# A small clock of step times sets the order inside three mixers; gate products move ahead in the queue; weight slabs are halved

## The reference

```python
for l in range(2):                                     # first block: two hybrid layers
    h = layer_norm(ALPHA*x + 0.5*swiglu(x, ffn1), ...)
    q,k,v,b,a,z, sw_q,sw_k,sw_v, xa_q, gates = split(h @ w_in)
    o_dn = gated_delta_rule(...)                       # 4 heads, chunks, triangular solve, state chain
    o_sw = sliding_window_attention(...)               # 8 heads in 4 pairs, window 128, sink logits
    o_xa = memory_cross_attention(...)                 # 4 heads over 256 memory rows
    merged = sum_n sigmoid(gates_n) * (branch_n @ w_branch_n)
    h = layer_norm(ALPHA*h + merged @ w_out)
    x = layer_norm(ALPHA*h + 0.5*swiglu(h, ffn2))
x = x + token_mixer(rmsnorm(x))                        # second block: four attentions, 4 heads each:
                                                       # stick-breaking (sb), blocks with T5 bias (mb),
                                                       # forgetting (fx), top-256 keys (ds)
x = x + conv_ffn(rmsnorm(x)); out = rmsnorm(x)
```

## Time and profile before

| | us |
|---|---|
| median of 3 runs | 3833.05 (3832.97 to 3834.43) |
| the profiled execution: its own time | 3830.93 |
| its span, first to last instruction | 3829.2 |
| PE busy | 3677.4 (96%) |
| DVE busy | 1879.4 (49%) |
| ACT busy | 1383.5 (36%) |
| mean granted TensorE clock | 0.981 |

### The profile page before, as it was taken

How to read it: one execution, slowest core, us unless ns; L and a number is a source line. 1 busy time by engine, 2 the same in 40 slices (tenths; PEclk the granted TensorE clock), 3 DMA queues, 4 the chain that set the end, 5 groups by cost and what they waited for, 6 DMA issues and landing times.

```text
span 3829.2 us, 42473 instructions
## 1 busy us (share of the span) xinstructions
PE 3677.4 (96%) x16966; PEld 2905.5 (76%) x16966; DVE 1879.4 (49%) x3117; ACT 1383.5 (36%) x2292; POOL 0.2 (0%) x4
## 2 busy tenths in 40 slices
PE   8999989999999999999899999999999998999998
PEld 6888768777778887888688768788857676778887
DVE  4333575563543344334665654533254567646643
ACT  4332363442242223222644432422234333334432
POOL 0000000000000000000000000000000000000000
PEclk9999999999999999999999999999989999999999
DMA  4322210112222222222110112222222112122222
GB/s 152 121 99 95 81 61 34 44 56 83 86 85 94 94 94 83 94 94 93 66 45 23 67 61 94 77 99 91 97 76 74 55 61 77 67 88 88 96 97 77
DMA packets 88316, 308.26 MB, mean 81 GB/s; under 512 B 9846, under 2 KB 12055, under 8 KB 87992
## 3 DMA queue, kind: packets, MB, share of 16 engines
q1 hardware_dynamic: 88120, 305.55, 23.0%
HBM read 300.80 MB, written 4.72 MB: 80 GB/s over the span
## 4 chain that ended last, share of the span: by engine, by line
PE 86%; DVE 8%; ACT 4%; issue 1%; DMA 0%; DVEq 0%; SPq 0%; ACTq 0%
PE bank L1569 25%; PE bank L1570 25%; PE bank L1571 25%; PE bank L1552 4%; PE bank L1604 1%; DVE page_f L2329 1%; PE bank L1557 1%; DVE w_lo L2153 1%; PE bank L1579 1%; ACT w_hi L1826 1%; ACT L1810 0%; PE bank L1624 0%; DVE small L2277 0%; PE bank L1779 0%; ACT page_f L1973 0%
## 5 line engine op out<-in xcount | busy, mean ns | idle before, releaser
L1569 PE MATMUL bank<-page_r,w_hi 128*128 128x512 f32 (+1 forms) x4488 | 1817.5, 405 | 50.0 <-DVE page_r L2184 26.6
L1570 PE MATMUL bank<-page_r,w_hi 128*128 128x512 f32 (+1 forms) x4488 | 1768.9, 394 | 0.0
L1571 PE MATMUL bank<-page_r,w_lo 128*128 128x512 f32 (+1 forms) x4488 | 1768.5, 394 | 0.0
L1569 PEld LDWEIGHTS bank<-page_r,w_hi 128*128 128x128 f32 x4488 | 850.1, 189 | 274.5 <-issue 69.3
L2153 DVE TENSOR_TENSOR w_lo<-raw,w_hi 128x1024 fp32r<-128x1024 f32 x561 | 685.6, 1223 | 696.9 <-ACT w_hi L1826 696.8
L1571 PEld LDWEIGHTS bank<-page_r,w_lo 128*128 128x128 f32 x4488 | 849.2, 189 | 199.0
L1570 PEld LDWEIGHTS bank<-page_r,w_hi 128*128 128x128 f32 x4488 | 850.7, 190 | 186.1 <-issue 4.6
L1826 ACT ACTIVATE w_hi<-raw 128x1024 fp32r<-128x1024 f32 x561 | 590.7, 1054 | 792.8 <-PE bank L1571 791.1
L2253 DVE TENSOR_TENSOR page_f<-page_f,bank 128x512 f32<-128x512 f32 x88 | 60.6, 689 | 261.4 <-PE bank L1571 255.0
L1898 ACT ACTIVATE page_r<-page_f 128x512 fp32r<-128x512 f32 x88 | 55.7, 633 | 354.4 <-DVE page_f L2253 354.4
L1552 PEld LDWEIGHTS bank<-page_f 128*128 128x128 f32 x1344 | 165.1, 193 | 14.5 <-DVE page_f L2422 4.2
(11 more groups left out here) (212 smaller groups left out, 2216.5 us busy)
## 6 DMA issues: line engine op xcount, KB each, us to landing
raw<-weights SPq DMA_DIRECT2D x561, 512.0 KB, 3.2
page_f<-x_t SPq DMA_DIRECT2D x8, 256.0 KB, 4.3
bias_rows<-page_f SPq DMA_DIRECT2D x8, 256.0 KB, 2.0
page_f<-bias_rows SPq DMA_DIRECT2D x8, 256.0 KB, 3.3
out_t<-page_f SPq DMA_DIRECT2D x8, 256.0 KB, 2.1
cst<-consts SPq DMA_DIRECT2D x1, 1088.0 KB, 6.9
page_f<-mem_t SPq DMA_DIRECT2D x8, 128.0 KB, 5.6
bias_rows<-page_f SPq DMA_DIRECT2D x8, 64.0 KB, 1.9
```

Of the source, the lines that this page charges most:

```text
L1569: self.e.matmul(o, hi, X.hi[kt], start=first, stop=False)
L1570: self.e.matmul(o, hi, X.lo[kt], start=False, stop=False)
L1571: last = self.e.matmul(o, lo, X.hi[kt], start=False, stop=final)
```

## The change

1. **Slabs of 4 blocks.** 1122 slabs of 128x512. Six raw buffers, four rounded ones. The remainder is written over the raw slab (`w_lo` is the same memory as `raw`), so a raw buffer is free only when PE has multiplied its slab, and SP waits for that. Rounding of slab s+3 stands at block 1 of slab s, its remainder at block 2, the load of slab s+5 at block 0. Pages go from 76 to 84.
2. **A clock.** Each yield now returns an estimate: PE time, a list of DVE and ACT times, and whether the next step needs the result. `Pace` keeps the time of PE (`now`) and of DVE and ACT (`free`). `weave` takes a lane whose next step is ready by `now` plus 0.1, else a ready step of the queue, else whatever is ready first. A yield may also return a flag or another generator to wait for, so each lane goes on by itself.
3. **No common ends.** Hybrid: lane one is decays, head 0, head 2, cross heads 0-1; lane two head 1, head 3, window pairs 0-1; cross heads 2-3 start after head 2, window pairs 2-3 after head 3. Second block: a lane for each head pair goes through sb, mb, fx, ds; the ranking is a lane. All projections but the first four are queue work.
4. **Gates.** The delta output gates are products of the queue before the heads end, and `gate_ahead(n)` puts the eight gate products of a merge into the queue ahead of it, so the last merge has only its branch products (32 blocks) left.

```diff
-NSLAB = 561
-NRAW = 3
-NSPLIT = 3
-AHEAD = NSPLIT - 1
-PAGES = 76
-N_SB, N_MB, N_FX, N_DS = 2.4, 1.9, 2.3, 1.8
+SLAB = 4
+NSLAB = 1122
+NRAW = 6
+NHI = 4
+AHEAD = NHI - 1
+PAGES = 84
+BLOCK_US = 0.7
+LAG_US = 0.1
...
+def vec(width, n=1):
+    return (("V", 0.06 + width / 760),) * n
+def act(width, n=1):
+    return (("S", 0.2 + width / 1200),) * n
+def mat(width, n=1):
+    return 0.0017 * width * n
+BLOCK_LOAD = (("V", 0.17), ("S", 0.15))
...
+    def tell(self, w):
+        took = w.step()
+        if w.done:
+            if w in self.queue:
+                self.queue.remove(w)
+        elif isinstance(took, tuple):
+            tensor, others, waits = took
+            t = self.now = max(self.now, w.ready) + tensor
+            for engine, us in others:
+                t = self.free[engine] = max(t + LAG_US, self.free[engine]) + us
+            w.ready = t + LAG_US if waits else 0.0
+        else:
+            w.needs = took
...
+    def weave(self, gens):
+        works = [Later(g) for g in gens]
+        self.start()
+        while works:
+            w = self.next_of(works, self.now + LAG_US) or self.from_queue(self.now + LAG_US)
+            if w is None:
+                w = self.next_of(works + self.queue, math.inf)
+            self.tell(w)
+            works = [w for w in works if not w.done]
...
-            if j == ROUND_AT:
-                self.rounded(s + AHEAD)
-            if j == REST_AT:
-                self.rested(s + AHEAD)
+            if j == 0:
+                self.loaded(s - 1 + NRAW)
+                self.rested(s + AHEAD - 1)
+            if j == 1:
+                self.rounded(s + AHEAD)
+            if j == 2:
+                self.rested(s + AHEAD)
...
-            yield
+            yield BLOCK_US * n / SEQ, BLOCK_LOAD, False
...
+        bg.weave([first_lane(), second_lane(), branches(), third_lane(), fourth_lane()])
...
-        go(mg.add(2, joined(OX)))
+        while bg.queue:
+            bg.steps(1)
         go(mg.add(1, joined(OS), final=True))
...
+        bg.weave([lane(0), lane(1), logits(), ranking(), branches()])
...
     def load_slab(self, s):
         if s >= NRAW:
-            self.wait_ge(self.m.s_hi, s - NRAW + 1)
-            self.wait_ge(self.m.s_lo, s - NRAW + 1)
+            self.wait_ge(*self.freed[s - NRAW])
```

More of the change, by code:

```diff
@@ L248, in beside @@
                 self.steps(1)
-    def weave(self, gens, n, longer=None):
-        gens, owed = list(gens), 0.0
-        while gens:
-            if longer is not None and not longer.done:
-                longer.step()
-            for g in list(gens):
-                try:
-                    k = next(g)
-                except StopIteration:
-                    gens.remove(g)
-                    continue
-                owed += n if k is None else k
-                self.steps(int(owed))
-                owed -= int(owed)
+    def weave(self, gens):
+        works = [Later(g) for g in gens]
+        self.start()
+        while works:
[4 more added lines that the diff above has]
+            works = [w for w in works if not w.done]
 def bc(ap):
@@ L993, in head, with output_gates, finish @@
         outs[h] = (o, k["o"])
-    def finish(self, l, X, outs):
+    def output_gates(self, l, X, gates):
+        for h in range(4):
+            b = yield from self.product(("w_in", l), 13 + h, X)
+            z = self.pages.take()
+            k = self.marks("gate").will(scalar="tanh", vector="silu")
+            self.output_gate(k, b, z)
+            self.banks.give(b, k["silu"])
+            gates[h] = (z, k["silu"])
+            yield 0, act(SEQ) + vec(SEQ), False
+    def finish(self, l, outs, gates):
         O, work = {}, {}
@@ L1018, in finish @@
             self.pages.give(q, k["scale"])
[L1019 to L1023 removed]
+            k.will(vector="times")
+            self.finish_gate(k, z, z_ready, o)
             self.pages.give(z, k["times"])
@@ L1222, in hybrid_mixer, with conv_of @@
-        self.bg.weave([crosses(0), windows(0), crosses(2), windows(2)], 1)
+        bg = self.bg
+        w_in = ("w_in", l)
+        def conv_of(m):
+            b = yield from self.product(w_in, m, X)
+            return (m, *self.short_conv(l, m, b))
+        ba, *convs = feed(source, [self.project_n(w_in, 12, X, 8)] + [conv_of(m) for m in (0, 4, 8)])
+        D = self.marks("decay")
+        cols = {x: self.small(16) for x in ("be", "hbe", "g", "gc", "ngc", "eg", "beg")}
+        qkv, gates, outs, OX, OS = {}, {}, {}, {}, {}
@@ new lines, in third_lane, with fourth_lane, branches @@
+        def third_lane():
+            yield heads[2]
+            yield from crosses((2, 3))
+        def fourth_lane():
+            yield heads[3]
+            yield from windows((2, 3))
+        def branches():
+            for f in heads:
+                yield f
+            yield gated
+            O = yield from self.finish(l, outs, gates)
+            bg.add(mg.add(0, O))
+            mg.gate_ahead(2)
+            for f in crossed:
+                yield f
+            bg.add(mg.add(2, joined(OX)))
+            mg.gate_ahead(1)
@@ L1324, in second_block @@
-        merges.append(bg.add(mg.add(2, joined(OFX))))
-        while not keys.done:
-            keys.step()
-            bg.steps(2)
-        tbs = self.bias_tiles(range(4, 8))
-        dq, dk = [bg.get(x) for x in dq], bg.get(dk)
-        vd = lambda h, kb: (nar.f[:, kb * P:kb * P + 64], nar_ready, slice(64 * (h % 2), 64 * (h % 2) + 64))
-        bg.weave([self.causal_softmax(j, dq[j], dk, vd, dsa(tbs), ODS) for j in range(2)], N_DS)
-        for p, _ in [dk] + pen[1:] + list(tbs.values()):
-            self.pages.give(p, *soft_ends())
@@ L1334, in second_block, with forget, f @@
-        self.pages.give(nar, *soft_ends(), (self.lanes["keys"].vector, self.lanes["keys"].raised[2]))
-        for m_ in merges:
-            bg.get(m_)
+        def forget(rows):
+            def f(_, h, i, L):
+                p, ready = rows[h]
+                own = self.pages.take()
+                kr = self.marks("fox").will(vector="minus causal")
+                self.fox_bias(kr, p, ready, own, cc[:, 4 * i + h:4 * i + h + 1], k["cc"], L)
+                return [(own.cols(L), kr["causal"])], own
+            return f
@@ L1511, in add @@
                 self.part(m - 1)
+            yield 0, vec(SEQ, 2), False
         o.drop(O, b.full)
```

547 lines of the change are left out of this document (293 added, 254 removed).

## The result

| | before | after |
|---|---|---|
| median, us | 3833.01 (4 runs, 3832.97 to 3834.43) | 3860.19 (4 runs, 3858.97 to 3861.56) |
| ratio | 1 | 1.007 (95% interval 1.0053 to 1.0088) |
| span of the profiled execution | 3829.2 | 3859.3 |

What follows compares the result with a forecast made beforehand. The kernel was taken as bound by PE, busy 3677.4 of 3829.2 us. From 3830.9: -80 (mixers), +3 (last merges), +3 (hand-overs), -2 (start) gave 3754.9; with 2.1 for the median, 3757 us, range 3705 to 3808.

Steps and rivals of the forecast that it cites:

- Reading of the bound: Whole kernel: bound by PE; nearly all an order can give back, 160.8 us, lies in the three mixers.
- Part 3, slabs of 4: Slab work throughout: added DVE and ACT time lies beside PE; +3 us for stage hand-overs, -2 at the start.
- Rival C: Mixers: slab remainders come late in bursts behind lane steps, making the kernel slower, 3877 us; chance 0.09.
- Its 95 waits of 1.3 us: Mixers: remainders late at a quarter of about 380 slabs, 124 us lost against 80 gained.
- Part 1, hybrids: Hybrid mixers: clock and lanes fill PE's gaps with queue work, less 15 us of new waits for each mixer.
- Pool: Three mixers: idle and slow-clock time that can go, 122.3 us of 160.8 after unchanged work ahead of the weave.
- The new waits: Mixer lane steps issued early by short clock estimates: 15 us per hybrid, 12 in the second mixer, 42 together.
- cover doesn't run out: Hybrid mixer: 485 us of PE work meets a lane's chain of about 250 us, 394 at most.
- Part 1, second mixer: Second mixer: clock and lanes win back idle and slow-clock time, less the norms' 22.5 us and 12 of new waits.
- Part 2: Last merges: gates moved ahead leave four blocks per tile, PE and DVE level; +1 us per mixer, 0 to 6.
- Table loads: ACT in a hybrid mixer: 13 to 20 loads expected, up to 9 us more per mixer, beside PE.
- The signs named beforehand: Right: mixer idle about 35 to 20 us, no feed-forward over 2 us longer; wrong: w_lo among PE's three largest waits.

Runs made afterwards that it cites:

- slab8_all: new_order_slab8 with the clock told of ACT's product copies, each head's finish and the three convolutions at the hybrid start; 3791.7 us.
- slab8_late: new_order_slab8 with the last merge's gates put back into the merge in each mixer; 3793.8 us.
- in8_best: in8_ready with merge 2's gates queued before the finish, and without gate_ahead(3) for the second block's last merge; 3764.2 us.
- new_pairs: The change with six rounded and eight raw buffers, the work of two slabs placed together every second slab; 3813.2 us.
- new_order_slab8: The change with the slabs of 8, buffers and placing of the kernel before; 3789.0 us.
- slab8_start: new_order_slab8 with the clock told of the three convolutions still in the lists when a hybrid weave starts; 3797.1 us.
- new_hi6: The change with six rounded and eight raw buffers, slab work done two slabs earlier; 3815.7 us.
- slab8_ready: new_order_slab8 with the clock told of ACT's copy of each product and of each head's finish; 3767.3 us.
- in8_ready: slab8_ready with the remainder written over the raw slab as in the change, 80 pages; 3777.4 us.
- in8_consts: in8_ready with the load of constants issued behind x tile 5 in place of behind all eight; 3775.0 us.
- old_order_slab4: The kernel before, with its old order, given the change's slabs of 4, buffers, placing and pages; 3904.6 us.

## Why the prediction was wrong

- **Reading of the bound, right.** What an order can give back lay in the mixers; no experiment in the order alone moved a feed-forward by more than 1.5 us.
- **Part 3, slabs of 4: the step that failed.** It stood at +3 -2 = +1 us, bounds -6 to +12, and measured +71 (70 in the old order). The durations were right, and so was the start (-2.4). No run shows the 3 us put on the hand-overs by themselves; the five norm hand-overs alone have 25 waits more, some 25 us. The error is the sentence that the additions "lie beside PE and cost nothing by themselves". It compared busy shares of whole windows. At a hand-over PE waits for each tile, and there the slab work isn't beside the chain but in it, through the order of two lists: a mean of 2.66 us a tile became 3.99, against 2.8 that PE needs. The row that gave it away was in the earlier trace rows, the 5.3 us for L2184, with the norm timeline behind it, and I didn't lay that timeline out. The second half is supply: the prediction named it ("a DVE backlog of that length would stop PE") and then compared only the shortest distance, 10 blocks against 11, and looked for backlogs in the mixers only. They were there, 6.3 us of waits each, and behind the feed-forwards' shift chain as well; two slabs more ahead gave back 10 to 12 us a hybrid and 5.2 a feed-forward. The wait of SP for PE was weighed for the slabs' landing, not for what stands behind it in SP's list: the constants.
- **Rival C** had w_lo among the three largest waits, as measured (39.7 us), but its cause, lane steps put back to back by the new weave, was not the cause: the kernel with the old order loses as much, and its w_lo waits in hybrid mixer 0 are 8.0 us against 6.3 in after. So its sign came true, and its 3877 was nearer than the forecast, but mostly by luck. Its 95 waits of 1.3 us in the mixers were not there; there are 11 on w_lo in the whole kernel.
- **Part 1, hybrids: sized wrong.** Pool less new waits was some 81 - 30 = 51 us for the two; the order alone gave 2.5. The new waits that were priced, from the hop that the clock has too short, didn't come: the fp32 products (L1552, L1679 in after) have no row at all among PE's waits in after, where before had 5.1 us. What mattered were products of the queue that a lane needs: the code marks them done when they are in the lists, and the prediction took that for a plain dependency. Telling the clock gave 21 us. The claim that cover doesn't run out (485 us against 250 to 394) was right as a sum over the mixer and wrong in time: slab8_all's empty queue at 735 to 810, while 131 weight blocks were multiplied after the mixer's last other product.
- **Part 1, second mixer: right, and larger.** 29 us expected, 46 measured. The waits of 9.5 us (L2291) and the row on L1903 of the earlier trace rows are gone. Some 7 us of the 46 may not be the order's but the clock's at the norm, see the last section.
- **Part 2.** The last merges were put at +1 each, bound 6. In the hybrids the gates ahead are no cost (without them, in slab8_late, each mixer is 4 us longer); in the second block they cost +5.1, near the bound, and in8_best takes it back.
- **Table loads** stayed at 13 in hybrid mixer 0, the low end. The Trainium skill, "ScalarE: Activation LUTs", section "Rules for kernel authors", budgets about 2.7 us for a switch of sets; the trace of after shows 1.283 us for each of the thirteen loads, as the earlier trace rows did, and 1.31 us from the end of ACT's instruction before a load to the start of the one behind it, at the median of all 42. The trace decides. No wait of PE names a load.
- **The warning of the Trainium skill on many small tiles** ("VectorE: DVE Perf Modes", section "The TRN2 errata") was priced as +90 us if all of it lay on the path, and set aside. It spoke against the right part. But most of what the runs show isn't DVE's extra time: new_pairs has the same 1122 remainders and hands back 8.9 of the 11.9 us that a feed-forward lost.
- **The signs named beforehand.** w_lo among PE's three largest waits came true, for slower. Of those for right, the second mixer's idle time fell (35 to 16 us), while the hybrids' rose from 35 to 45 us and each middle feed-forward grew by 11 to 12 us, not at most 2.

## What to carry to other kernels

Weigh added instructions by the chain they stand in, not by the engine's idle share: where one engine feeds PE tile by tile, write out a period of all lists and compare it with PE's time for the tile. A model that orders work must know of every instruction that makes an input, also of a copy that stands elsewhere in a list, and must start from the backlog that is there. Cover has a time: count the blocks left in the queue when the long chain comes, before filling early waits. And measure two independent halves of a change apart before anything else: here one was worth -46 us and the other +71.

## What was not expected of the hardware

The same code at the second mixer's norm ran at different mean granted clocks in different kernels. The first 44 us of that stage in new_order_slab8:

```profile
2816.00:2860.00 44.00, 33.81 (x88) 17.52 (x87) 23.27 (x40) 23.34 (x42) 0.00 (x0) 0.84 0.21 71
```

and in slab8_start, whose code is the same there:

```profile
2822.00:2866.00 44.00, 37.80 (x58) 15.45 (x58) 19.22 (x34) 21.16 (x38) 0.00 (x0) 0.59 0.16 57
```

That is 88 matmuls against 58 in the same time, at 0.84 and 0.59 of the full clock. The kernel before had 0.65 in these 44 us, after 0.88. The mixers differ by 7 us (526.6 against 533.9). Read the same way over the kernels with the new order, the clock goes with the length of the mixer: 525.6 to 526.6 us where it is 0.84 to 0.88 (after, new_hi6, new_order_slab8, slab8_ready), 528.8 and 528.9 at 0.69 (in8_ready, in8_consts), and 531.3 to 533.9 where it is 0.58 to 0.65 (the other nine). In the old order it does not show: old_order_slab4 has 0.88 there and a mixer of 573.9 us, the kernel before 0.65 and 572.6, but the two differ in their slabs as well. The executions of new_order_slab8 fall into two groups, 3784.1 twice and 3793.9 and 3795.5, which fits, but only one execution, of the faster two, was profiled. What decides was not found. A difference under 10 us between two of these kernels can be this alone, so it is read by stage.
